# Bias rows of a dilated attention stage: one fp32 product replaced by two fp32r products over a doubled one-hot matrix

## What is computed

```
rel = blk + jnp.arange(blk)[:, None] - jnp.arange(2 * blk)[None, :]
band = (rel >= 0) & (rel <= blk)
bucket = _t5_bucket(jnp.clip(rel, 0, blk) * dilation)
bias = jnp.transpose(bias_table[bucket], (2, 0, 1))
...
logits = jnp.where(valid[None, :, None, None], s + bias[None, None, None], NEG_INF)
```

## Time and profile before

| what | value |
|---|---|
| median of three runs | 1884.37 us (1882.8 to 1886.26) |
| the profiled execution: its own time | 1886.68 us |
| its span in the trace | 1884.9 us |
| PE busy | 1873.7 us, 99% of the span |
| DVE busy | 1144.4 us, 61% |
| ACT busy | 632.6 us, 34% |
| granted clock of PE, mean | 0.997 of full speed |

### The profile page before, as it was taken

How to read it: one execution, slowest core, us unless ns; L and a number is a source line. 1 busy time by engine, 2 the same in 40 slices (tenths; PEclk the granted TensorE clock), 3 DMA queues, 4 the chain that set the end, 5 groups by cost and what they waited for, 6 DMA issues and landing times.

```text
span 1884.9 us, 24357 instructions
## 1 busy us (share of the span) xinstructions
PE 1873.7 (99%) x9024; PEld 1555.2 (83%) x9024; DVE 1144.4 (61%) x1475; ACT 632.6 (34%) x862; POOL 138.8 (7%) x140
## 2 busy tenths in 40 slices
PE   9999999999999999999999999999999999999998
PEld 6888888888888888888888888888888888888887
DVE  7787778776666444585642354366777786324533
ACT  6313344344333233344322232223333443222321
POOL 0011002300000011002000000100010120000000
PEclk9999999999999999999999999999999999999999
DMA  4222222333333334222323343322222223333332
GB/s 167 68 79 90 79 67 79 101 101 95 95 100 93 96 113 132 79 79 93 112 93 98 109 126 99 103 90 73 79 74 73 62 79 113 101 99 91 99 101 68
DMA packets 54654, 176.49 MB, mean 94 GB/s; under 512 B 5875, under 2 KB 12291, under 8 KB 54572
## 3 DMA queue, kind: packets, MB, share of 16 engines
q1 hardware_dynamic: 49296, 170.82, 28.9%
q10 hardware_dynamic: 4764, 3.41, 0.8%
q0 software_dynamic: 512, 1.08, 0.2%
HBM read 172.09 MB, written 2.13 MB: 92 GB/s over the span
## 4 chain that ended last, share of the span: by engine, by line
PE 98%; DVE 2%; DMA 0%; issue 0%; ACT 0%; SPq 0%; DVEq 0%
PE ps L539 31%; PE ps L540 30%; PE ps L541 30%; PE ps L1002 1%; PE ps L547 1%; PE ps L1031 1%; PE ps L1014 1%; PE ps L1032 1%; PE ps L804 1%; PE ps L794 0%; DVE wlo L1471 0%; DVE yr L1490 0%; PE ps L1045 0%; DMA raw<-wst 0%; PE ps L879 0%; DVE h L2093 0%
## 5 line engine op out<-in xcount | busy, mean ns | idle before, releaser
L539 PE MATMUL ps<-xhi,whi 128*128 128x512 f32 x1576 | 623.6, 396 | 1.8 <-DVE xlo L1477 1.3
L541 PE MATMUL ps<-xlo,whi 128*128 128x512 f32 x1576 | 615.5, 391 | 0.0
L540 PE MATMUL ps<-xhi,wlo 128*128 128x512 f32 x1576 | 615.1, 390 | 0.0
L1471 DVE TENSOR_TENSOR wlo<-raw,whi 128x1024 fp32r<-128x1024 f32 x317 | 407.8, 1286 | 217.7 <-ACT whi L1155 217.1
L1155 ACT ACTIVATE whi<-raw 128x1024 fp32r<-128x1024 f32 x317 | 333.8, 1054 | 543.5 <-PE ps L541 482.5
L539 PEld LDWEIGHTS ps<-xhi,whi 128*128 128x128 f32 x1576 | 296.8, 188 | 66.5 <-DVE wlo L1471 3.1
L541 PEld LDWEIGHTS ps<-xlo,whi 128*128 128x128 f32 x1576 | 296.5, 188 | 62.9
L540 PEld LDWEIGHTS ps<-xhi,wlo 128*128 128x128 f32 x1576 | 297.0, 188 | 59.4 <-issue 0.2
L539 PE MATMUL ps<-mh,whi 128*128 128x512 f32 (+1 forms) x528 | 202.3, 383 | 0.0
L540 PE MATMUL ps<-mh,wlo 128*128 128x512 f32 (+1 forms) x528 | 202.1, 383 | 0.0
L541 PE MATMUL ps<-mh,whi 128*128 128x512 f32 (+1 forms) x528 | 202.0, 383 | 0.0
(11 more groups left out here) (331 smaller groups left out, 1975.6 us busy)
## 6 DMA issues: line engine op xcount, KB each, us to landing
raw<-wst SPq DMA_DIRECT2D x317, 512.0 KB, 3.5
h<-xT SPq DMA_DIRECT2D x8, 256.0 KB, 6.0
out<-h SPq DMA_DIRECT2D x8, 256.0 KB, 2.3
oP<-oB POOLq DMA_DIRECT2D x16, 66.0 KB, 2.1
bias_a<-bias_rows ACTq DMA_DIRECT2D x4, 256.0 KB, 4.6
bias_b<-bias_rows ACTq DMA_DIRECT2D x4, 256.0 KB, 4.6
wsf<-wsT ACTq DMA_DIRECT2D x1, 512.0 KB, 3.5
bsb<-bs ACTq DMA_DIRECT2D x1, 512.0 KB, 4.4
```

Of the source, the lines that this page charges most:

```text
L539: pe.matmul(o, w[0], x[0], start=first, stop=False, **kw)
L540: pe.matmul(o, w[1], x[0], start=False, stop=False, **kw)
L541: return pe.matmul(o, w[0], x[1], start=False, stop=done, **kw)
L1471: dve.tensor_tensor(wlo[:, n % SLOTS, :], raw[:, n % 2, :], whi[:, n % SLOTS, :].bitcast(F32), ALU.subtract).then_inc(s_split, 1)
```

## The change

The product is taken in fp32r. The table is split into a high and a low part, and both are put as stationary operand `rbr` into a tile of 97 partitions: the high part in partitions 0 to 32, the low part in 64 to 96, zeros between. The three groups stand in column blocks of 32, so their results come out in partitions 0, 32 and 64 of the banks. The one-hot matrix is stored twice in its constant, with 31 rows of zeros between, so that one product over 97 partitions adds both parts. It is now loaded as 97 x 1024 and rounded on the chip into `ohr`. Two products of 512 columns take the place of four of 256.

```
-                ohs = sb("ohs", [33, 24 + 4 * 256], F32, m2)
+                ohs = sb("ohs", [97, 24 + 4 * 256], F32, m2)
+            ohr = dpt[0:97, 0, :, :].rearrange("p a c -> p (a c)")
+            rbr = dpt[0:97, 1, 0, 0:P]
...
-                pe.wait_ge(s_dld, 32)
-                pe.wait_ge(s_bdv, 1)
-                for g in range(4):
-                    grp = max(0, g - 1)
-                    ins = pe.matmul(bank(2 + g // 2)[0:8, (g % 2) * 256:(g % 2) * 256 + 256], ohs[:, 8 * grp:8 * grp + 8],
-                                    ohs[:, 24 + g * 256:24 + (g + 1) * 256], start=g % 2 == 0, stop=True, skip_group_check=True)
+                pe.wait_ge(s_bhi, 1)
+                pe.wait_ge(s_boh, 1)
+                for n in range(2):
+                    ins = pe.matmul(bank(2 + n), rbr, ohr[:, n * T:(n + 1) * T], start=True, stop=True)
...
                         for m in range(first):
                             up_unit(m, bank(THIRD_BANK if m == 2 else (A0[up] + m) % 2))
+                            if m == 1:
+                                dve.wait_ge(s_dld, 32)
+                                dve.wait_ge(s_bdv, 2)
+                                groups = ohs[0:33, 0:24].rearrange("p (g c) -> p g c", c=8)
+                                b_hi, b_lo = (rbr[32 * r:32 * r + 33, :].rearrange("p (g c) -> p g c", c=32)[:, 0:3, 0:8]
+                                              for r in (0, 2))
+                                split(b_hi, b_lo, groups, s_bhi)
+                            if m == 3:
+                                dve.tensor_copy(ohr, ohs[:, 24:]).then_inc(s_boh, 1)
...
-                            dve.tensor_copy(fsb[:, :], bank(2, 2)[0:8, :]).then_inc(s_bdv, 1)
+                            dve.tensor_copy(fsb[:, 0:T], bank(2)[0:8, :])
+                            dve.tensor_copy(fsb[:, T:T + 256], bank(3)[32:40, 0:256])
+                            dve.tensor_copy(fsb[:, T + 256:], bank(3)[64:72, 256:T]).then_inc(s_bdv, 1)
...
+            dve.memset(rbr.bitcast(F32), 0.0).then_inc(s_bdv, 1)
             dve.memset(ohs[32:33, 0:24], NEG).then_inc(s_bdv, 1)
...
-    return out.reshape(33, 1024)
+    out = out.reshape(33, 1024)
+    return np.concatenate([out, np.zeros((31, 1024), np.float32), out], 0)
```

More of the change, by code:

```diff
@@ L502, in build @@
         s_bld = sem("bias_loaded")
+        s_bhi = sem("bias_weights_split")
+        s_boh = sem("bias_one_hot_rounded")
         s_bmm = sem("bias_rows_multiplied")
@@ L1372, in mlp @@
                         if layer == 0:
-                            act.wait_ge(s_bdv, 2)
+                            act.wait_ge(s_bdv, 3)
                             act.dma_start(fdram, fsb).then_inc(s_fst, 16)
```

## The result

The changed kernel takes 1891.49 us, median of six runs (1890.88 to 1892.72), against 1884.38 us for the kernel before (1882.8 to 1886.26): 7.1 us more, a ratio of 1.0041 with a 95% interval of 1.003 to 1.0051. Another five runs, later, gave 1892.22 against 1884.6, 1.0038 (1.0024 to 1.0051). It is slower, by about what was forecast. The profiled execution took 1892.35 us, its span is 1890.2.

The account below looks back on a forecast made before the run. PE was taken to bound the kernel, 98% of the last chain. Saving -1.5, stall +7.3 and clock +1.5 gave +7.3 us: profiled execution 1886.68 to 1894.0, median 1884.37 to 1891.7, range 1882 to 1899.5.

Parts of the forecast that it names:

- The mechanism: One DMA engine carries all 97 one-hot rows, landing at 912.1; DVE waits behind unit 1 and PE's unit 4 starts late.
- The stall: At unit 4 of `up00`, PE waits for DVE, which waits for the load: 7.3 us late, bounds 2.8 to 20.
- the clock: After the stall PE's granted clock may fall to 1.2 GHz: 1.5 us, bounds 0 to 3.2.
- PE's saving: At the bias rows, two fp32r products replace four float32 ones: 1.5 us saved, bounds 1.3 to 2.0.
- the issue: Issue of the one-hot load on ACT, 1.62 us before, may grow; counted 0, with 1.3 us of PE kept for the range.
- The memset: On DVE ahead of `lo` at 895.09, 97 x 128: a few tenths of a us, within 1.04 us of slack.
- the rounding: On DVE after `up_split(3)`, rounding the 97 x 1024 one-hot: 1.2 us, hidden because DVE's round is shorter than PE's.
- the three copies: Three copies instead of one of 1.21 us, moving the same columns: 1.2 to 1.6 us in all, covered.
- the weight units' turns on the engine: Two weight units' packets alternate with the one-hot's on its single DMA engine, delaying its landing by 2.6 us.
- (a): Rival: load not queued on one engine, or landed by 904.8; only PE's saving left, 1882.9 us; chance 0.18.
- (b): Rival: ACT's queue held until the load's packets are taken, about 909.8; 15 us stall, 1899.4 us; chance 0.10.
- (c): Rival: one DMA engine moves a packet in 0.28 us, so PE stalls 20 us; 1904.4 us; chance 0.08.

Follow-up runs that it names:

- e1: Changed kernel with 15 more rows of zeros, so the one-hot load has 112 rows instead of 97; 1883.79 us, ratio 0.9997 to the kernel before.
- e5: Changed kernel with 9 more rows of zeros, so the one-hot load has 106 rows instead of 97; 1883.64 us, ratio 0.9997 to the kernel before.
- e6: Changed kernel with 128 rows in the one-hot load instead of 97; 1882.46 us, ratio 0.9992 to the kernel before.
- e2: Changed kernel with DVE's wait for the loads and the table split moved from behind unit 1 to behind unit 3; 1882.25 us, ratio 0.9995.
- e3: Changed kernel with DVE's wait for the loads and the table split moved from behind unit 1 to behind unit 2; 1887.35 us, ratio 1.0017.
- e4: Kernel before, its four float32 products and late wait kept, with only the one-hot load grown from 33 to 97 rows; 1883.15 us, ratio 0.9996.
- e7: Kernel before, its float32 products kept, with the 97-row load and DVE waiting for the loads behind unit 1; 1892.42 us, ratio 1.0042.

## Why the prediction was right

**The mechanism** was right in each link: one engine (one completion packet), the landing long after, DVE idle ahead of the CAST on `dpt`, PE idle ahead of unit 4, a clock at its lower level. e1, e5 and e6 vary the number of engines, e2 and e3 the place, e4 and e7 take load and wait apart. The completions are 11, 1, 2, 16 and 16 for 33, 97, 106, 112 and 128 rows, each time the largest divisor up to 16. The Trainium skill, "DMA: Bandwidth & Descriptors", section "Why a DMA increments its semaphore by 16 and not by 1", states that rule for the outer dimension of both sides of a transfer, and these counts agree with it.

**The terms.** The stall was put at 7.3 and measured 7.03; the clock at 1.5 and measured 1.78; PE's saving at 1.5 and measured 1.44 to 1.55. The sum was +7.3, the stage shows +7.4, the median +7.1. Some of that is luck, since errors inside the stall cancel. The first packets moved about a us earlier than I let them, because the issue, which I feared would grow, shrank from 1.62 to 0.53 us. From there to DVE's going on were 19.6 us (890.2 to 909.8) and not 16.0 + 2.6 + 0.3 = 18.9, so 0.7 more. And 0.3 for the two tiny splits was 0.41 with their gaps (909.80 to 910.21). The packets themselves were 0.16 us apart, as I had it (25 of them in the 4 us from 904.9 to 908.9). The +7.3 was meant for the profiled execution, 1886.68 to 1894.0, and that came to 1892.35: it has the 7.4 in the stage, but one early stretch at the lower clock where before has two, and so reaches the stage 1.9 us sooner. How many of them an execution has moves every median by up to as much, and that the one of +7.1 lies so close to the sum is luck too.

**The covers.** The memset took 0.17 us, the rounding 0.69 (I took 1.2), the three copies 0.67 + 0.42 + 0.42 = 1.51 instead of 1.21. All stayed hidden, as e1 shows: with the landing mended its up part is that of before.

**What I missed.** I counted the weight units' turns on the engine as a delay of the one-hot, but wrote that the weight transfers themselves go on. They took twice their time. In the changed kernel that lies behind the longer wait; in e2 it is 0.9 us. The turns explain 8 x 0.16 = 1.3 us of the 3.4 that a unit lost; why the shared engine came to a unit's packets so late besides stays open. My number for e3 missed something else: the turns of a third unit, which delay the one-hot again.

**The rivals.** (a) described not the changed kernel but e1 and e6: where the load lands in time the stage keeps PE's saving (88.00 and 87.99 against 89.45), though the medians can't tell it. (b) is out: the issue did not hold ACT. (c) is out as well: the load ran at 23 to 28 GB/s, 0.15 to 0.18 us a packet; the 0.28 of the earlier trace rows, read off three packets per engine, did not carry over to a queue of 97.

## What to carry to other kernels

Look at the row count of a transfer before its bytes: what counts is its largest divisor up to 16, and a handful of rows of zeros can make a load land four times sooner than the exact shape (4.8 us after its issue with 112 rows of 4 KB; with 97, DVE went on after 20.5). A load whose waiter comes late can be free however slow it is, as in e4, unless what it delays on its engine runs out of slack, as in e2; when a wait is moved forward to an engine that feeds the bottleneck, its landing time has to be worked out anew, and so do the transfers that share its DMA engine. And a gap of 7 us on PE costs more than itself, here 1.8 to 2.2 us more.

## What the runs showed of the hardware that I had not expected

- One 97-packet load on one DMA engine doubled the time of weight units that use all 16 (3.4 to 6.8 us, up to 7.9): the unit was through on its other engines 3 us before it was on the one it shared, and landed with that one.
- The issue of the one-hot on ACT's queue took 1.62 us with 33 rows, 0.53 with 97 and with 106, 1.70 with 112 and 1.38 with 128. It follows neither the rows nor the number of engines alone. Its cause stays open; nothing here depended on it.
- After a gap of 3.4 us the granted clock still read 1.00 and the matmuls were back at 0.24 us by the second; after gaps of about 7 us it read 0.50, and seven intervals of 0.43 us followed in one run and nine in two others. The loss is 1.8 us in the first, and 0.2 more for each further one.
